# Exponentials behind block copies, a third tile abreast, whole rotations on VectorE, and an earlier split, in a fp32 transformer kernel of one core

## What is computed

```python
# first block, for each of two layers
proj = h @ w_in[l]                       # 21 tiles of 128 columns with padding
mixed = concat(nsa_mixer(...), gla_mixer(...), pool_mixer(...))
h = layer_norm(ALPHA * h + mixed @ w_out[l])
h = layer_norm(ALPHA * h + square(relu(h @ w_up[l])) @ w_down[l])

# in nsa_mixer: keys and queries are rotated (partial_rope), two masked softmaxes
# (selected blocks, window) of q @ k.T and one over compressed keys, each times values

# second block, for each of two layers (mixer A in the first, mixer B in the second)
h = h + 0.5 * rms_norm(swiglu(rms_norm(h, g0)), g1)
h = h + rms_norm(mixer(rms_norm(h, g2)), g3)       # B: 16 query heads, 4 key heads, rotated
h = h + 0.5 * rms_norm(swiglu(rms_norm(h, g4)), g5)
h = h + rms_norm((p[i] @ ple_proj[i]) * sigmoid(rms_norm(h, g6) @ ple_gate[i]), g7)
```

## Time and profile before

| | |
|---|---|
| median of 3 runs | 3416.29 us (3415.85 to 3416.61) |
| the profiled execution | 3416.2 us, its span 3414.4 us |
| PE busy | 3334.5 us, 98% |
| VectorE, ScalarE, GpSimd busy | 1834.6, 1243.7, 342.3 us |
| mean granted clock of TensorE | 0.994 of full speed |

### The profile page before, as it was taken

How to read it: one execution, slowest core, us unless ns; L and a number is a source line. 1 busy time by engine, 2 the same in 40 slices (tenths; PEclk the granted TensorE clock), 3 DMA queues, 4 the chain that set the end, 5 groups by cost and what they waited for, 6 DMA issues and landing times.

```text
span 3414.4 us, 43051 instructions
## 1 busy us (share of the span) xinstructions
PE 3334.5 (98%) x16830; PEld 2654.4 (78%) x16830; DVE 1834.6 (54%) x2932; ACT 1243.7 (36%) x1878; POOL 342.3 (10%) x244
## 2 busy tenths in 40 slices
PE   9999999999999999999999999999999999999997
PEld 6767888776688887888777778887788876788886
DVE  5766334567653446443666664435644367654436
ACT  3354223424442324332333342324433235533324
POOL 0310000212100020000233100000000012000001
PEclk9999999999999999999999999999999999999999
DMA  4102222311122222223322122232222321122232
GB/s 163 62 32 75 98 94 99 129 63 50 50 81 98 99 93 87 98 93 105 113 74 69 62 84 95 98 105 93 87 98 95 103 94 44 57 105 97 97 109 73
DMA packets 81433, 300.39 MB, mean 88 GB/s; under 512 B 9040, under 2 KB 9040, under 8 KB 80640
## 3 DMA queue, kind: packets, MB, share of 16 engines
q1 hardware_dynamic: 78624, 284.20, 24.4%
q0 software_dynamic: 1568, 11.98, 0.9%
q10 hardware_dynamic: 1088, 2.10, 0.2%
HBM read 296.14 MB, written 2.10 MB: 87 GB/s over the span
## 4 chain that ended last, share of the span: by engine, by line
PE 88%; DVE 6%; ACT 3%; issue 1%; POOL 1%; DMA 0%; ACTq 0%; DVEq 0%; POOLq 0%
PE bank L874 25%; PE bank L876 25%; PE bank L875 25%; PE bank L918 2%; PE bank L925 2%; PE bank L919 2%; DVE wl L2038 1%; PE bank L1419 1%; ACT sc L1722 1%; PE bank L1181 1%; PE bank L1431 1%; PE bank L1196 1%; PE bank L1162 1%; ACT wh L1561 1%; PE bank L1120 1%
## 5 line engine op out<-in xcount | busy, mean ns | idle before, releaser
L874 PE MATMUL bank<-x,wh 128*128 128x512 f32 x2632 | 1054.4, 401 | 11.5 <-DVE h L2482 5.7
L876 PE MATMUL bank<-x,wl 128*128 128x512 f32 x2632 | 1027.9, 391 | 0.0
L875 PE MATMUL bank<-x,wh 128*128 128x512 f32 x2632 | 1027.0, 390 | 0.0
L1561 ACT ACTIVATE wh<-raw 128x1024 fp32r<-128x1024 f32 x528 | 558.9, 1059 | 1157.4 <-PE bank L876 1087.6
L2038 DVE TENSOR_TENSOR wl<-raw,wh 128x1024 fp32r<-128x1024 f32 x528 | 677.3, 1284 | 553.1 <-ACT wh L1561 551.8
L874 PEld LDWEIGHTS bank<-x,wh 128*128 128x128 f32 x2632 | 495.2, 188 | 132.3 <-issue 25.7
L876 PEld LDWEIGHTS bank<-x,wl 128*128 128x128 f32 x2632 | 495.2, 188 | 105.7
L875 PEld LDWEIGHTS bank<-x,wh 128*128 128x128 f32 x2632 | 496.1, 188 | 98.2 <-issue 3.4
L874 PE MATMUL bank<-mid,wh 128*128 128x512 f32 x1216 | 474.9, 391 | 0.5 <-DVE wl L2038 0.5
L875 PE MATMUL bank<-mid,wh 128*128 128x512 f32 x1216 | 473.1, 389 | 0.0
L876 PE MATMUL bank<-mid,wl 128*128 128x512 f32 x1216 | 473.1, 389 | 0.0
(11 more groups left out here) (342 smaller groups left out, 3332.6 us busy)
## 6 DMA issues: line engine op xcount, KB each, us to landing
raw<-stream SPq DMA_DIRECT2D x528, 512.0 KB, 3.2
raw_apart<-stream SPq DMA_DIRECT2D x10, 512.0 KB, 3.5
sm<-small POOLq DMA_DIRECT2D x2, 2144.0 KB, 10.6
tb<-tab POOLq DMA_DIRECT2D x2, 1728.0 KB, 14.8
h<-x_t ACTq DMA_DIRECT2D x4, 512.0 KB, 6.8
out_t<-h SPq DMA_DIRECT2D x8, 256.0 KB, 2.1
tba<-tab_a POOLq DMA_DIRECT2D x1, 1152.0 KB, 7.7
pf<-p_t POOLq DMA_DIRECT2D x2, 512.0 KB, 5.0
```

The costliest lines, as they stand in the source:

```text
L874: pe.matmul(dst, hi, src[:, kc, 0, :], start=start, stop=False)
L875: pe.matmul(dst, hi, src[:, kc, 1, :], start=False, stop=False)
L876: return pe.matmul(dst, lo, src[:, kc, 0, :], start=False, stop=stop)
L1561: act.activation(high_of(n)[:, :], raw_of(n)[:, :], ACT.Copy).then_inc(hi_done, 1)
```

## The change

The exponentials in steps of three blocks: `plan_n` gives none of them behind the first block's copy, one behind the second's, three behind the third's (before: two, one, one). Layer 1's first mixer starts with a third tile two chunks behind the two abreast; all side work placed up to piece 54 comes five pieces later there; its unit 0 brings no split, and both engines do one more split at the end of layer 0's second FFN instead. VectorE does the rotation of Q0 + 2 (unit 20, both layers) and those of k0 and q0 in mixer B as a whole, with GpSimd left out. The embedding's first `emb_splits` moves from chunk 2 to chunk 1, in both layers.

```diff
-BY_ONE, BY_TWO, BY_THREE, GATED = together(1), together(2), together(3, 2), together(3, 4)
+BY_ONE, BY_TWO, BY_THREE, GATED = together(1), together(2, 2), together(3, 2), together(3, 4)
...
-            yield from PLACED.get(at, ())
+            yield from PLACED.get(at if order == BY_ONE or at > 59 else at - 5, ())
...
-            k = -(-len(parts) * (n + 1) // len(groups)) - (-(-len(parts) * n // len(groups)))
-            for i in range(k):
-                yield parts[-(-len(parts) * n // len(groups)) + i]
+            if t == 2:
+                yield from parts[(0, 0, 1)[n]:(0, 1, 4)[n]]
+            else:
+                yield from parts[-(-len(parts) * n // len(groups)):-(-len(parts) * (n + 1) // len(groups))]
...
-                        if k in ROPED:
+                        if k in ROPED and k < N_PROJ - 1:
...
-                        if B_TILES[k][0] != "v":
+                        if B_TILES[k][0] != "v" and k < 3:
+                            c.tick("rope")
+                        elif B_TILES[k][0] != "v":
...
-                if n < len(order):
+                if n < len(order) and m < 2:
...
-                        split()
+                        if layer == 0 or k:
+                            split()
...
-                    split(layer + 2 if m == DC - 1 else 1)
+                    split(3 if m == DC - 1 else 1)
...
-                                dve.stream_shuffle(proj[:, SPARE[ROPED[k]], :], src, SWAP)
-                                free(dve.tensor_tensor(proj[:, ROPED[k], :], src, tb1[:, T_COS:T_COS + S], ALU.mult))
+                                rt, ap = proj[:, SPARE[ROPED[k]], :], proj[:, ROPED[k], :]
+                                shuffled = dve.stream_shuffle(rt, src, SWAP)
+                                if k == N_PROJ - 1:
+                                    link(shuffled)
+                                free(dve.tensor_tensor(ap, src, tb1[:, T_COS:T_COS + S], ALU.mult))
+                                if k == N_PROJ - 1:
+                                    link(dve.tensor_tensor(rt, rt, tb1[:, T_SIN:T_SIN + S], ALU.mult))
+                                    settled()
+                                    dve.wait_ge(rope_done, 6 * layer + 5)
+                                    dve.tensor_tensor(ap, ap, rt, ALU.add).then_inc(rope_done, 1)
...
-                    split(layer + 1 if m == DC - 1 else 1)
+                    split(2 if m == DC - 1 else 1)
...
+            def roped_whole(dst, src):
+
+                k = c.n.get("roped", 0)
+                dve.wait_ge(rotated, k)
+                rt = prod[k % 2][:, :]
+                link(dve.stream_shuffle(rt, src, SWAP))
+                free(dve.tensor_tensor(dst, src, tbb[:, B_COS:B_COS + S], ALU.mult))
+                link(dve.tensor_tensor(rt, rt, tbb[:, B_SIN:B_SIN + S], ALU.mult))
+                settled()
+                dve.tensor_tensor(dst, dst, rt, ALU.add).then_inc(rotated, 1)
+                c.tick("roped")
...
+                            elif k < 3:
+                                roped_whole(b_home(k)[:, :], src)
...
-                    if k in (2, 4):
+                    if k in (1, 4):
```

## The result

The changed kernel takes 3423.1 us (median of 20 runs, 3418.4 to 3430.8) against 3416.2 for the kernel before (20 runs, 3413.1 to 3418.9), a ratio of 1.0021, 95% interval 1.0015 to 1.0027: slower by 6.9 us, where 3413.6 was forecast. Half of its times lie at 3418 to 3422 and half at 3424 to 3431; the profiled execution (3420.1 us, span 3418.2) is of the lower half. One execution each of e5, e9, e14 and the kernel before was disturbed and took over 1000 us longer; the ranges and ratios leave these out, the medians do not (0.5 us in e5's, 0.1 or less in the others').

A forecast was written before the change was run, and what follows sets the result against it. TensorE, busy 98% of the span, was taken as the bound, so only its 80 us idle could matter. Terms -5.8 - 1.8 - 1.9 + 3.5 + 1.0 + 0.9 + 1.5 = -2.6 us from 3416.2 gave 3413.6, range 3410 to 3417.5.

The forecast's parts named there:

- Side work five pieces later in layer 1: Layer 1's first mixer: nearly all only moves, but the window comes late for the compression; +0.9 us (0 to +1.5).
- Gate's third split: Both embeddings: split one chunk sooner removes two 2.05 us waits and the slow clock behind the second; -5.8 us.
- Mixer B: Two whole rotations on VectorE let PE's first scores start sooner; -1.8 us (bounds -0.6 and -2.9).
- Third tile abreast: Start of layer 1: a third tile fills PE's idle time while VectorE's norm delivers chunks; -1.9 us (-1.0 to -3.0).
- ScalarE's third split: End of layer 0's second FFN: split awaits its DMA and delays square(7), +3.5 us; slow clock behind it, +1.0.
- Exponentials and whole rotation: Softmax steps: copy waits return at the scaling and mixed chunks' low part, +0.3; slow clock +1.2; together +1.5 us.
- the clock falls at each longer wait: Rival: half clock follows waits at the norm, mixed chunks and step 11, and stays in mixer B; 3421.9 us, chance 0.15.

The follow-up runs named there:

- e5: Kernel before plus third tile abreast and side work five pieces later, ScalarE's third split left behind square(7): 5.5 us over before, ratio 1.0021.
- e9: Whole change, but layer 1's first mixer's side work from piece 37 on in its old place: 3414.0 us, 0.9995 of the kernel before.
- e14: Whole change, but gate work and first decay at their old pieces, window's group still five late: 3416.6 us, 0.9998 of the kernel before.
- e1: Kernel before plus third tile abreast, with the early third split and side work five pieces later: 3425.6 us, ratio 1.0035.
- e6: Kernel before plus third tile abreast and early third split, side work from piece 37 on in its old place: 2.6 us over before, ratio 1.0008.
- e7: Kernel before plus third tile abreast, without early third split, side work from piece 37 on unmoved: 1.5 us under before, ratio 0.9996.
- e4: The changed kernel run again unaltered, for a second profile and more times: 3428.2 us, 1.0029 of the kernel before.
- e3: Kernel before plus only the gate's third split one chunk sooner: 3410.3 us, ratio 0.9982.
- e11: Kernel before plus only the two whole rotations on VectorE in mixer B: 3414.7 us, ratio 0.9997.
- e8: Kernel before plus only the new order of exponentials and copies on ScalarE in three-block steps: 3419.1 us, ratio 1.0010.
- e13: Whole change, but the window's group back at its old pieces, gate work and first decay five late: 3415.9 us, 0.9998 of the kernel before.

## Why the prediction was wrong

The step that failed is "Side work five pieces later in layer 1", taken at +0.9 with bounds 0 and +1.5: e9 sets it at 9.1 (medians), e1 against e6 at 6.8, e5 against e7 at 7.0, and by the ratios all three pairs are between 8.5 and 9.2. Two things were missing in it.

First, only the window was walked through. Among what "only moves" was the first decay, from piece 37 to 42: from ahead of unit 4 to behind it. Unit 4's rotation runs on GpSimd right behind that unit, and VectorE's split and decay now run beside it. The rows of before show what that did not touch; the decay there is done before the rotation starts:
```profile
683.70 0.68 DVE L2217 SCALAR_TENSOR_TENSOR proj<-proj,gt 128x512 f32<-128x512 f32 x1
...
687.57 2.19 POOL L760 TENSOR_TENSOR proj<-proj,tb 128x512 f32<-128x512 f32 x1 [39.92 <-DVE proj L2401]
```
And after:
```profile
691.57 1.81 DVE L2042 TENSOR_TENSOR wl<-raw,wh 128x1024 fp32r<-128x1024 f32 x1 [0.64 <-ACT wh L1564]
692.38 2.15 POOL L762 TENSOR_TENSOR proj<-proj 128x512 f32<-128x512 f32 x1
...
696.98 0.63 ACT L1708 ACTIVATE gt<-gt 128x512 f32<-128x512 f32 x1 [5.44 <-DVE gt L2227]
697.52 1.05 ACT L1564 ACTIVATE wh<-raw 128x1024 fp32r<-128x1024 f32 x1
698.60 1.23 DVE L2042 TENSOR_TENSOR wl<-raw,wh 128x1024 fp32r<-128x1024 f32 x1 [1.05 <-ACT wh L1564]
...
702.88 0.69 DVE L2415 COPY proj<-bank 128x512 f32<-128x512 f32 x1
```
The split takes 1.81 in place of 1.22 and the decay 1.77 in place of 0.68, 1.7 us more. Then comes a detour over ScalarE: its exponential for the end of the decay (1708) waits 5.44 us for VectorE, unit 5's high part stands behind it, and VectorE idles another 1.05 us for that. VectorE passes the delay on to the second decay, and unit 6's copy starts at 702.88, 2.4 us after PE ended that unit (its last matmul starts at 700.06 and takes 0.39); the forecast had 0.5. So 0.9 became 2.75. With the decay back in place (e14) the wait is 0.86, so the move of the decay makes the other 1.9; how much of that is GpSimd and how much the detour was not tried apart. The gate work has no part in it: it ends on VectorE near 689.4 in both. e14's 0.86 is the forecast's own number for the move it had looked at, with luck in its working: the 696.2 taken for unit 6's end is the start of VectorE's turned copy, and PE ended that unit only at 696.7 (ScalarE's split starts at 696.75), but PE's own turning, 0.5 us, moves in ahead of the compression as well, and the two cancel. The prediction knew such slow instructions from its rows (a split of 2.00, a low part of 1.76 beside GpSimd), but did not ask which of the moved ones would get beside GpSimd. The Trainium skill (SBUF — State Buffer, "Who interferes with whom") says that a VectorE instruction with two inputs in SBUF contends with a GpSimd one that reads SBUF; the trace agrees, 1.77 against 0.68 us for the same decay.

Second, no slow clock was put behind this wait. The forecast put one behind the waits at the norm and in step 11, not here, where it reckoned with a wait of 0.9; behind e14's 0.86 indeed none came. At 2.7 it came in all four profiles (after, e1, e4, e5), and in e4's it stayed for 24 us. The rule of the clock that the prediction weighed was right in kind here: 24 us at half clock would lose 12, and 10.3 were lost. What runs in that stretch is the compression, matmuls of 64x32 between pieces of dense work. That these keep the clock down was not tried, and what decides between 1.4 and 10.3 us in one and the same kernel stays open.

The other steps, in their order:
- *Gate's third split*, -5.8: measured -5.9 (e3), both waits and the slow stretch gone.
- *Mixer B*, -1.8: measured -1.7 (e11), not told from nothing. In the traces the first wait falls from 5.28 to 3.87, by 1.4. The next wait, for a scaling, is 1.50 to 1.86 in kernels with the edit and 1.10 to 1.83 in those without it, so what it gives back is within a few tenths and isn't settled.
- *Third tile abreast*, -1.9: -1.8 in the stage of e7, -1.5 in the medians.
- *ScalarE's third split*, +3.5 and +1.0: the chain came as written, issue at 647.81, landing 3.3 later, split, square(7) at 652.03, PE 3.0 us idle, slow first tiles: +4.0 in the stage, +4.1 in the medians (e6 less e7).
- *Exponentials and whole rotation*, +1.5: the waits stand where they were put (3.48 at piece 168, 1.85 in step 11). Measured +4.3, the order 3.4 of it and the rotation 0.5. The prediction put the waits at +0.3 and the slow clock at +1.2. The waits are the term that is surely too small: PE idles 3.5 us more in the steps of e8's profile at the same mean clock, though part of that idle time lies inside slow stretches, so the steps are only 1.7 longer, 1.6 of it in layer 1. The rest of the 3.4 is not located.

Of the rivals, "the clock falls at each longer wait" (3421.9) came nearest, 1.2 under the median, but mostly by luck. It names the norm, the mixed chunks, step 11 and mixer B, not the compression, where most of the loss is; e9 has all its waits and takes 3414.0.

## What to carry to other kernels

When a block of side work is shifted by n pieces, list for every item what it crosses on each engine, not only the item with the nearest deadline: an item that changes sides with another engine's long operation changes its own duration. Then price the wait that results together with the clock behind it. Here, against e9's stage of 124.4 us, the wait of 0.86 cost 1.1, and that of 2.7 cost 4 or 13. And try the parts of a change that packs several ideas by themselves: the gate's split, mixer B and the bare third tile give -9.4 together, and the rest of the change costs 16.

## What the runs showed of the hardware

The granted clock after a wait is not fixed by the wait. The same wait of 2.7 us was followed by some 3.5 us of half clock in one execution of the changed kernel and by 24 in another; waits of 0.30 and 0.86 us at the same matmul (e13, e14) by none. Where the slow stretch falls in the softmax steps varies too: in e7 the stretch behind step 2's wait of 1.94 us is missing and lies behind the low part's wait, which is then 2.82 and not 1.29, and layer 0's steps take 114.5 against 113.5 us. So I infer that in the kernel before part of the slow stretch lay in time that PE would otherwise have waited for the low part. PE in e7:
```profile
179.59 0.66 PE L1185 MATMUL bank<-ident,sc 128*128 128x128 f32 x4 [1.94 <-ACT pt L1735]
...
190.79 0.77 PE L878 MATMUL bank<-x,wh 128*128 128x512 f32 x1 [2.82 <-DVE x L2058]
```
